# Hybrid decoder step on one core: last tile in half sums, index lists by tile group, third expert's load after the first gathers

## What is computed

```python
mix = jnp.concatenate([y_a, y_b.reshape(bt, s, W_B)], axis=-1) @ w_out
x = layer_norm(DEEPNORM_ALPHA * x + mix, ln1_g, ln1_b)
x = layer_norm(DEEPNORM_ALPHA * x + grouped_moe(x, ...), ln2_g, ln2_b)
# grouped_moe: router scores -> best group of 4 experts -> its top 2 -> gates
for e in range(N_EXPERTS):
    h = jax.nn.silu(xt @ w_gate[e]) * (xt @ w_up[e])
    out = out + comb[:, e:e + 1] * (h @ w_down[e])
```

## Time and profile before

| | us |
|---|---|
| median of 3 runs | 1237.67 |
| lowest, highest | 1236.41, 1237.78 |
| the profiled execution's own time | 1235.54 |
| its span in the trace | 1233.9 |
| TensorE busy | 1173.8 (95%) |
| VectorE busy | 887.6 (72%) |
| ScalarE, GpSimd busy | 528.7, 481.8 |

### The profile page before, as it was taken

The page is one execution under the profiler, slowest core; times in us unless marked ns, Lnnn a source line. Parts: engine busy times, 40 slices in busy tenths (PEclk is TensorE's granted clock), DMA queues, the critical chain, the costliest instruction groups (busy, mean ns, idle before and its releaser), DMA issues.

```text
span 1233.9 us, 23637 instructions
## 1 busy us (share of the span) xinstructions
PE 1173.8 (95%) x7100; PEld 984.5 (80%) x7101; DVE 887.6 (72%) x1911; ACT 528.7 (43%) x870; POOL 481.8 (39%) x591
## 2 busy tenths in 40 slices
PE   7999999999989989999998989999999999999976
PEld 7999999978868847888786968787878888788842
DVE  4466798568879767477876767777777777777766
ACT  4132211111103472233332346666666666666666
POOL 3106873100131116234242125555445555445446
PEclk9999999999999999999999789999999999999988
DMA  8689895685448673476697649899988889756496
GB/s 244 218 289 276 286 260 150 166 261 196 173 148 275 214 265 125 149 260 224 253 340 294 247 171 291 263 313 271 317 254 280 251 256 312 184 117 172 88 322 256
DMA packets 138840, 290.87 MB, mean 236 GB/s; under 512 B 49650, under 2 KB 67138, under 8 KB 127508
## 3 DMA queue, kind: packets, MB, share of 16 engines
q1 hardware_dynamic: 120404, 226.10, 52.5%
q0 software_dynamic: 17328, 61.80, 21.1%
q10 hardware_dynamic: 1040, 2.10, 0.5%
HBM read 178.49 MB, written 111.46 MB: 235 GB/s over the span
## 4 chain that ended last, share of the span: by engine, by line
PE 52%; DVE 3%; ACT 3%; issue 2%; POOL 1%; DMA 1%; ACTq 0%; DVEq 0%; POOLq 0%
PE p_out L2813 21%; PE p_out L2837 11%; PE p_out L2096 10%; PE p_x1t L2798 3%; PE p_parts L2761 1%; DMA xg<-x_rows,g_idx 1%; PE p_x1t L2107 1%; PE p_out L2144 1%; PE p_parts L2822 1%; ACT junk L2717 1%; PE p_out L2878 1%; PE p_parts L2117 1%; POOL mixt_low L1801 1%; PE p_router L2783 1%; PE p_out L2128 0%
## 5 line engine op out<-in xcount | busy, mean ns | idle before, releaser
L2518 DVE TENSOR_TENSOR wgu<-w_raw,wgu (+1 forms) x192 | 229.8, 1219 | 99.7 <-ACT wgu L2640 67.0
L2813 PE MATMUL p_out<-wgu,xg_high 128*128 x768 | 246.7, 403 | 5.4 <-issue 4.3
L2640 ACT CAST wgu<-w_raw x188 | 192.8, 1052 | 55.2 <-issue 52.4
L2813 PEld LDWEIGHTS p_out<-wgu,xg_high 128*128 128x128 f32 x768 | 140.3, 190 | 42.5 <-issue 16.3
L2813 PE MATMUL p_out<-wgu,xg_low 128*128 x384 | 151.4, 394 | 0.0
L2401 POOL TENSOR_TENSOR spare_e<-nothing 128x1 f32<-128x1 f32 x48 | 44.3, 922 | 212.1 <-DVE yo L2537 212.1
L2402 POOL DMA_INDIRECT acc_rows<-yo,si x48 | 112.8, 2350 | 9.1 <-issue 9.1
L2096 PE MATMUL p_out<-w_out_high,mixt_high 128*128 128x512 f32 x240 | 95.5, 398 | 0.0
L2096 PE MATMUL p_out<-w_out_high,mixt_low 128*128 128x512 f32 x240 | 94.3, 393 | 0.0
L2096 PE MATMUL p_out<-w_out_low,mixt_high 128*128 128x512 f32 x240 | 94.1, 392 | 0.0
L2813 PEld LDWEIGHTS p_out<-wgu,xg_low 128*128 128x128 f32 x384 | 72.5, 189 | 15.7
(11 more groups left out here) (507 smaller groups left out, 2844.2 us busy)
## 6 DMA issues: line engine op xcount, KB each, us to landing
w_raw<-in_w_gate SPq DMA_DIRECT2D x16, 1024.0 KB
w_raw<-in_w_up SPq DMA_DIRECT2D x16, 1024.0 KB
wd_high<-w_down_high SPq DMA_DIRECT2D x16, 1024.0 KB
wd_low<-w_down_low SPq DMA_DIRECT2D x16, 1024.0 KB
ya_u<-in_w_down SPq DMA_DIRECT2D x38, 256.0 KB, 4.4
w_down_low<-ya_r SPq DMA_DIRECT2D x38, 256.0 KB, 5.6
acc_rows<-ax SPq DMA_DIRECT2D x18, 512.0 KB, 6.8
xin<-in_x_prompt SPq DMA_DIRECT2D x16, 512.0 KB, 6.1
```

The lines of the kernel that those rows point to most:

```text
L2518: low = tt(wgu[:, slot, 1, at], raw[:, slot, at], wgu[:, slot, 0, at].bitcast(F32), ALU.subtract)
L2640: nc.scalar.copy(wgu[:, slot, 0, at], raw[:, slot, at]).then_inc(hi_set, 1)
L2813: mm = t.matmul(pg[b][:, :, :], x[:, b, k, :], w[h][:, k], start=(k == 0 and x is xh and h == 0), stop=(k == KD - 1 and x is xl))
```

## The change

Six edits:

1. For the last tile the output product raises a semaphore after each half (`o_half`, then `o_prod`), and VectorE does residual and statistics of a half as it comes (`sums`), then the norm. The seven identity products ahead of the last turn become ten.
2. `idle_products(30)` ahead of the counts becomes 28, `idle_products(32)` ahead of the list products 30, `idle_products(18)` behind them 16.
3. `rowhot` is made by tile group first and k second, and the list products go in the same order: tiles 0 to 8 for both k, then tiles 9 to 16 for both.
4. Two of the first expert's four low passes move ahead of VectorE's wait for the list, right behind the integer table of tile ends (L2493). The other two stay.
5. The third expert's load also waits until the first four gathers have landed.
6. `prep` is defined earlier, with the same text.

```diff
--- before.py
+++ after.py
...
@@ -2010,18 +2010,25 @@
                     ch.settle()
                     dve.sem_inc(gates_set, 1)
 
-                def residual(c, b, half, n=P):
+                def residual(c, b, half, n=P, halves=(0, 1)):
                     dve.wait_ge(z_in[b], (half + 1) * 16)
-                    dve.wait_ge(o_prod, c + 1)
-                    for m in range(2):
+                    if 1 in halves:
+                        dve.wait_ge(o_prod, c + 1)
+                    else:
+                        dve.wait_ge(o_half, 1)
+                    for m in halves:
                         cols = slice(m * SUP, (m + 1) * SUP)
                         v.scalar_tensor_tensor(z[0:n, b, cols], z[0:n, b, cols], ALPHA, po[b][m][0:n, :], ALU.mult,
                                                ALU.add).then_inc(z_set, 1)
 
-                def norm(c, b, first, half, n=P):
-                    dve.wait_ge(z_set, c * 2 + 2)
-                    for m in range(2):
+                def sums(c, b, n=P, halves=(0, 1)):
+                    dve.wait_ge(z_set, c * 2 + 1 + halves[-1])
+                    for m in halves:
                         ch.mark(v.bn_stats(st[0:n, b, m, :], z[0:n, b, m * SUP:(m + 1) * SUP]))
+
+                def norm(c, b, first, half, n=P, summed=False):
+                    if not summed:
+                        sums(c, b, n)
                     ch.settle()
                     v.memset(spare[:], 0.0)
                     ch(v.bn_aggr(ag[0:n, b, :], st[0:n, b]))
@@ -2078,8 +2085,10 @@
                         ch(v.tensor_scalar(i128[:], i128[:], 0.5, None, ALU.mult))
                     if c in CHOICES:
                         select(*CHOICES[c], c - 1)
-                residual(CH, 0, CH // 2)
-                norm(CH, 0, False, CH // 2)
+                for m in range(2):
+                    residual(CH, 0, CH // 2, halves=(m,))
+                    sums(CH, 0, halves=(m,))
+                norm(CH, 0, False, CH // 2, summed=True)
                 turn(CH, 0)
                 select(CH + 1 - SEL, SEL, CH + 1, True)
 
@@ -2095,8 +2104,7 @@
                             for x, w in PARTS:
                                 mm = t.matmul(po[b][m][0:n, :], mixt[x][:, b, k, 0:n], wo[w][:, k, m * SUP:(m + 1) * SUP],
                                               start=(k == 0 and x + w == 0), stop=(k == KD - 1 and x == 1))
-                    if 1 in halves:
-                        mm.then_inc(o_prod, 1)
+                    mm.then_inc(o_prod if 1 in halves else o_half, 1)
 
                 def turn(c, b, first, n=P):
                     pe.wait_ge(x1_set, c + 1)
@@ -2162,13 +2170,14 @@
                         turn(i * 2 + b - 1, (b + 1) % 2, False)
                         gather_parts(i * 2 + b - 2, False)
                 route(CH - 2, 0, False)
-                out(CH, 0, False)
+                for m in range(2):
+                    out(CH, 0, False, halves=(m,))
                 turn(CH - 1, 1, False)
                 gather_parts(CH - 2, False)
                 route(CH - 1, 1, False)
                 gather_parts(CH - 1, False)
                 pe.wait_ge(z_set, CH * 2)
-                for _ in range(7):
+                for _ in range(10):
                     t.matmul(po[1][0][:, 0:P], ident[:], ident[:], start=True, stop=True)
                 turn(CH, 0, False)
                 route(CH, 0, False)
@@ -2325,6 +2334,8 @@
                 sp.dma_start(x1_dram[LAST * P:SEQ, D:].rearrange("(t p) e -> p t e", p=P), comb[:, LAST:CH, :]).then_inc(comb_in, 16)
                 sp.dma_start(x1_dram[SEQ:, D:], comb[0:NS, CH, :]).then_inc(comb_in, 16)
                 sp.wait_ge(prep_done, 1)
+                for b in range(GS):
+                    sp.wait_ge(xg_in[b], 16)
                 gate_up(2)
                 for e in range(2):
                     down_landed(e)
@@ -2481,8 +2492,8 @@
                     tt(hot[:, k], i48[:].unsqueeze(1).broadcast_to(st_), tilef[:, k, :].unsqueeze(2).broadcast_to(st_),
                        ALU.is_equal).then_inc(hot_set, 1)
                 dve.wait_ge(rowf_set, 1)
-                for k in range(2):
-                    for lo, hi in ROW_PARTS:
+                for lo, hi in ROW_PARTS:
+                    for k in range(2):
                         sh = [P, hi - lo, P]
                         tt(rowhot[:, k, lo:hi], i128[:].unsqueeze(1).broadcast_to(sh),
                            rowf[:, k, lo:hi].unsqueeze(2).broadcast_to(sh), ALU.is_equal).then_inc(row_set, 1)
@@ -2491,6 +2502,15 @@
                 ch(tt(past[:], past[:], te[:], ALU.mult))
                 rd(of_tile[:, 1:2], past[:], axis=AX, op=ALU.max).then_inc(tile_set, 1)
                 ts(tab_e[:], te[:], 1.0, None, ALU.add).then_inc(te_set, 1)
+
+                def prep(i, slot, cs):
+                    for c in cs:
+                        at = slice(c * QG, (c + 1) * QG)
+                        dve.wait_ge(hi_set, i * 4 + 4 + c + 1)
+                        low = tt(wgu[:, slot, 1, at], raw[:, slot, at], wgu[:, slot, 0, at].bitcast(F32), ALU.subtract)
+                        low.then_inc(prep_done if c == 3 else low_set, 1)
+
+                prep(-1, 1, range(2))
                 dve.wait_ge(list_prod, 1)
                 ts(g_idx[:], p_ls[:, :], -1.0, 0.0, ALU.add, ALU.max).then_inc(lists_set, 1)
                 ts(lst[:], p_ls[:, :], -1.0, None, ALU.add).then_inc(lst_set, 1)
@@ -2510,13 +2530,6 @@
                         dve.wait_ge(xt_hi, i * 2 + h + 1)
                         low = tt(xl[:, b, part, :], pt_x[h], xh[:, b, part, :].bitcast(F32), ALU.subtract)
                     low.then_inc(xt_lo, 1)
-
-                def prep(i, slot, cs):
-                    for c in cs:
-                        at = slice(c * QG, (c + 1) * QG)
-                        dve.wait_ge(hi_set, i * 4 + 4 + c + 1)
-                        low = tt(wgu[:, slot, 1, at], raw[:, slot, at], wgu[:, slot, 0, at].bitcast(F32), ALU.subtract)
-                        low.then_inc(prep_done if c == 3 else low_set, 1)
 
                 def hidden(i, b, first, at):
 
@@ -2569,7 +2582,7 @@
                     ch(ts(tab_r[:], tab_r[:], 4, None, ALU.logical_shift_left))
                     v.memset(var2[:], 1.0).then_inc(te_set, 1)
 
-                prep(-1, 1, range(4))
+                prep(-1, 1, range(2, 4))
                 turn(0, 0)
                 for i in range(4):
                     step(i, i % 2, i // 2)
@@ -2761,7 +2774,7 @@
                         mm = t.matmul(pt_h[:, 0, :], ident[:], ident[:], start=True, stop=True)
                     mm.then_inc(spun, 1)
 
-                idle_products(30)
+                idle_products(28)
                 pe.wait_ge(chosen, len(CHOICES) + 1)
                 pe.wait_ge(cum_set, 1)
                 flat = msk[:].rearrange("p t e -> p (t e)")
@@ -2775,18 +2788,19 @@
                     mm = t.matmul(rest[:, c + 1:], ones2[:], msk[:, c:c + 1].broadcast_to([P, n, E]), start=False, stop=(c == TILES - 1))
                 mm.then_inc(cnt_prod, 1)
 
-                idle_products(32)
-                for k in range(2):
-                    for c in range(TILES):
-                        pe.wait_ge(hot_ids, c + 1)
-                        pe.wait_ge(row_set, 2 * k + (c >= ROW_PARTS[1][0]) + 1)
-                        mm = t.matmul(p_ls[:, :], rowhot[:, k, c], hot[:, k, c], start=(k + c == 0), stop=(k == 1 and c == TILES - 1))
+                idle_products(30)
+                for n, (lo, hi) in enumerate(ROW_PARTS):
+                    for k in range(2):
+                        for c in range(lo, hi):
+                            pe.wait_ge(hot_ids, c + 1)
+                            pe.wait_ge(row_set, 2 * n + k + 1)
+                            mm = t.matmul(p_ls[:, :], rowhot[:, k, c], hot[:, k, c], start=(k + c == 0), stop=(k == 1 and c == TILES - 1))
                 mm.then_inc(list_prod, 1)
                 pe.wait_ge(tile_set, 2)
                 for k in range(2):
                     mm = t.transpose(pg[1][0:1, k, 0:P], of_tile[:, k:k + 1], ident[:])
                 mm.then_inc(tile_turned, 1)
-                idle_products(18)
+                idle_products(16)
 
                 def turn(i, b, first):
 
```

More of the change, by code:

```diff
@@ L1681, in out_stage @@
             (row_in, wr_in, half_set, mix_high, mix_low, o_prod, z_set, var_set, rstd_set, x1_set, ax1_set, x1_turned, x1t_act,
-             x1t_dve, r_prod, r_set, sc_zero, ddch, rb_in, sel_set, consts, wo_high, wo_low, rq_prod, rq_set, fold_set, chosen, comb_set, dgch, raw_read, cum_set, gates_set) = sems("""row1_in wr_in half_set mix_high mix_low o_prod z_set var1_set
+             x1t_dve, r_prod, r_set, sc_zero, ddch, rb_in, sel_set, consts, wo_high, wo_low, rq_prod, rq_set, fold_set, chosen, comb_set, dgch, o_half, raw_read, cum_set, gates_set) = sems("""row1_in wr_in half_set mix_high mix_low o_prod z_set var1_set
```

(2 more changed lines are left out.)

## The result

| | before | after |
|---|---|---|
| median, us (6 runs each) | 1236.43 | 1230.24 |
| lowest, highest | 1235.96, 1237.78 | 1227.8, 1231.54 |
| profiled execution, its span | 1235.54, 1233.9 | 1230.92, 1229.3 |

The ratio is 0.9944, with a 95% interval of 0.9932 to 0.9957: 6.2 us, or 0.56%, faster.

A forecast was written before the change was run, and what follows sets the result against it. TensorE, busy 95% of the span, was taken as the bound, with waits, padding and low clock to gain from. 1.3 (front) + 5.9 (second gather) less 0.2 margin gave 7.0 us off 1237.67: 1230.7 us, range 1228.6 to 1235.1.

The forecast's parts named there:

- Second gather and third load: First gate/up: the 2.99 us stall for the second gather and the low clock behind it go, 5.9 us, bounds 4.5 to 6.0.
- Front term: Up to the first gate/up: first gather's turn 2.5 us earlier less 1.2 for low clock, 1.3 us, bounds 0 and 3.2.
- (a): Last tile: half sums make x1 ready 1.2 us earlier, but only 0.55 arrives at the turn behind ten identity products.
- s: How much earlier the index chain on VectorE runs: 1.0 us at the low clock to 2.2 at the high.
- (c): 28 idle products ahead of the counts: at the high clock they end near 686.3 and no longer bind.
- (d): turn(0,0) starts on the first gather, at 708.0 to 708.9 instead of 711.44, 2.5 to 3.4 us earlier.
- (e): TensorE standing before turn(0,0) brings a low clock into the first gate/up: charged 0 to 2.0 us, taken 1.2.
- The list's gain spent on the passes: Ahead of g_idx: the list's 2.1 us go to the two moved low passes; the table comes only s - 0.17 earlier.
- What is late next: After the stall: low half of tile 1 on VectorE, some 2.2 us behind the turn's end, covered by a 2.75 us half.
- Third load's slack: The third expert's load, issued 4 us later, is in by about 723, 5 us ahead of ScalarE's first cast.
- Rival 2: The second gather's issue stays 5.03 us whatever VectorE does; stall of 0 to 1, gain 6.0 us, 1231.7; chance 0.08.
- Rivals 1, 3 and 4: 1: low clock at first gather, 1233.2, chance 0.18; 3: only earlier index chain, 1236.1, 0.07; 4: late third load, 1241, 0.05.

The follow-up runs named there:

- hold only: The kernel before with only the wait for the four gathers ahead of the third expert's load added: 1231.82 us, ratio 0.9964.
- passes behind: The changed kernel with all four of the first expert's low passes behind the table, the wait for the gathers kept: 1229.12 us, ratio 0.9936.
- neither: The changed kernel with all four low passes behind the table and without the wait for the gathers: 1234.31 us, ratio 0.9983.
- no hold: The changed kernel without the wait for the four gathers ahead of the third expert's load: 1231.1 us, ratio 0.9957.
- late rows: The changed kernel with VectorE's add_rows (eight small operations) behind step 1 instead of step 0: 1228.11 us, ratio 0.9929.
- list by k: The changed kernel with row tables and list products in the order of before (k outermost): 1229.69 us, ratio 0.9934.
- seven: The changed kernel with seven identity products ahead of the last turn instead of ten: 1230.27 us, ratio 0.9933.
- all ahead: The changed kernel with all four of the first expert's low passes ahead of the table: 1232.11 us, ratio 0.9964.

## Why the prediction was right

Forecast 1230.7, measured 1230.24; forecast gain 7.0 of 1237.67, measured 6.2 (the kernel before came out at 1236.43 over more runs). The number was right partly by luck: a front that gains more than forecast at the high clock and a loss at the first down product that was not in the sum offset each other.

- **Second gather and third load: right, in size and cause.** Forecast 5.9, measured 6.0 (12.5 to 6.5 us between the first two gate/up products). Hold only, passes behind and neither show the cause: the load ahead of the gather. The prediction set the long issue beside it as a second cause; alone it makes no wait here (5.03 and 5.02 us in hold only and in passes behind, wait 0).
- **Front term: right in size for this trace, with other parts.** Forecast 1.3 with bounds 0 and 3.2; measured 1.8 from E in the trace of after and 3.4, a little beyond the upper bound, in those whose clock was high there (no hold, late rows: +40.8). Of its steps: (a) the 0.55 us of the half sums, with the ten products as what binds, came as worked out (+5.82) where the clock was high, and turned into a loss of 1.0 where it was low: 20 passes then took 4.11 us, not 2.5. I had put the low level only behind this place. (b) s was forecast 1.0 to 2.2; it was 0.6 in after and 2.2 in no hold and late rows. The latter is the high-clock case to 0.1 us. (c) The padding ahead of the counts no longer bound: 0.65 us of idle time before them in after and in no hold alike. (d) turn(0,0) started on the gather, after 1.89 us of idle time, and issue to turn took 4.5 us (4.5 to 4.8 in every trace in which that turn waits for the gather), not the 4.0 that I read from the end of its data. (e) The price of 1.2 us for a low clock in the first gate/up never came: the clock was high from 712 to 716 us in the trace of after and in all eleven of the experiments, although TensorE had stood up to 1.89 us before it.
- **The list's gain spent on the passes: right.** Forecast 2.1 us, 1.9 by list by k against no hold. g_idx follows the passes without a wait in after; the two passes cost 0.8 us of it beside a free place (passes behind).
- **"What is late next": wrong.** I named the low half of tile 1, which did come in time. What was late is `ht_low`: VectorE's hidden(0) runs behind two low passes (721.84, while silu ended at 720.86), add_rows stands behind it, then three passes, then `tail`. That chain is 6.7 us from hh to ht_low before and after alike. Before, the stall let VectorE finish its passes, and hh started 0.73 us behind the second gate/up; after, it started 1.56 us behind it, and the wait of the first down product grew from 1.35 to 2.19. A low clock under that product added 1.54 in the trace of after and in three of the seven others with this wait. That is the missing term of the sum: -0.84 us, and -2.4 with the low clock. Late rows shows it: with add_rows out of the chain the wait falls from 2.19 to 0.16.
- **Third load's slack: right.** Its first cast did not wait on it (728.38, after 0.22 us of idle time, with no transfer named as what ended it); SyncE issued it at 717.13 instead of 711.4, and the third gate/up of late rows and the two behind it ran without a wait on weights.
- **Rival 2 (the passes don't hold the gather): refuted** by 0.97, 2.54 and 5.03 us for the second gather's issue. Taken as a forecast for this issue, the Trainium skill's inference (SBUF — State Buffer, section "Who interferes with whom") that such subtractions don't delay the writing of descriptors failed. Whether it is the descriptors or the reading of the indices from SBUF that waits, no run here tells, so the inference itself is not refuted. **Rivals 1, 3 and 4** did not occur: no low clock in the first gate/up, no stall, no late weights.
- **The signs that I had named.** A g_idx with no idle time ahead of it, an issue of 2.54 us, no wait in the first gate/up and the second gate/up at 720.28 came as forecast. Three did not come in the trace of after: Turn(CH) was at 678.83 and not near 676.5, nt at 691.41 and not by 690.3, turn(0,0) at 710.39 and not by 709. g_idx was at 704.74, later than the 702.6 to 703.8 forecast, which I had called a sign of being wrong; counted from E it is +33.36 here, against +31.9 to +33.1 forecast, and +31.74 where the clock was high. And the lead did not stay the same: 7.1 us at the second gate/up, 4.6 at the end of the span.

## What to carry to other kernels

Hold a bulk load back until the small transfers that the next step needs have landed, and check what issues them: here the issue of the second indirect gather on GpSimd ended 0.85 us behind VectorE's last pass, and the load waited for that same pass, so the gather fell behind it. When a stall goes, follow every engine's queue from the point where it ended, small operations included, and not only that of the operand that was late: here eight tiny operations were worth 2 us beside the 6 of the whole change. Padding meant to keep the clock up took 1.7 times as long with a low clock over most of it (4.11 against 2.48 us for 20 passes), so a count that fits at the high level delays the work behind it at the low one.

## What was not expected of the hardware

The same code meets the low clock in different places in different executions. Behind the last output product TensorE is busy for 1.54 to 1.55 of 3 us in the traces compared (E + 0.5 to E + 3.5 in after, late rows, no hold, all ahead), and yet of the twelve traces with the change or a part of it five show a low clock between 674 and 680 us (after, hold only, seven, all ahead, neither) and the other seven do not; with ten products the turn then starts at +7.45 or at +5.8. That alone moves the front by 1.6 us (g_idx +33.36 in after, +31.75 in late rows and no hold), and it may be a part of why the runs of one kernel spread over 3.7 us, which single traces can't show. A gain of this size in one trace is no proof of the edit; the landmarks between which it should fall say more, where the clock between them is the same.
